# A one-core hybrid attention and retention block: sums of the first modulation tiles moved to TensorE, and wider feature jobs in the first half of the input projection

## The reference

```
mod = c @ w_ada + b_ada                        # (1, 2048) @ (2048, 6*2048): 100 MB of weights
sh1, sc1, gt1, sh2, sc2, gt2 = split(mod, 6)
h = rmsnorm(x, g_mix) * (1 + sc1) + sh1        # x is (256, 2048)
proj = h @ w_in                                # 2048 x 5376
qa, ka, va, qr, kr, vr, gr = split(proj)       # 1024, 128, 128, 1024, 1024, 1024, 1024 columns
ya = sliding_window_attention(qa, ka, va, sinks) * beta_attn
yr = silu(gr) * head_group_norm(retention(qr, kr, vr), g_ret)
x = x + gt1 * (concat(ya, yr) @ w_out)         # 2048 x 2048
h2 = rmsnorm(x, g_ffn) * (1 + sc2) + sh2
x = x + gt2 * (square(relu(h2 @ w1)) @ w2)     # 2048 x 8192, 8192 x 2048
return rmsnorm(x, g_final)
```

## Time and profile before

| | |
|---|---|
| median of 3 runs | 1197.4 us (1197.1 to 1199.3) |
| profiled execution, its own time | 1198.7 us |
| span from first to last instruction in it | 1196.9 us |
| TensorE busy | 1128.5 us, 94% |
| VectorE busy | 808.2 us, 68% |
| ScalarE busy | 490.6 us, 41% |
| mean DMA rate over the span | 253 GB/s |
| HBM read | 300.2 MB |
| TensorE's first product with `w_in` | starts at 67.6 us |

### The profile page before, as it was taken

One profiled execution on the slowest core, in us unless ns is written; L12 is line 12 of the kernel. 1 busy time (PEld: TensorE's weight loads), 2 busy tenths in 40 slices (PEclk: granted clock), 3 DMA queues, 4 the chain that ended last, 5 costly groups with the idle time before them and its releaser, 6 DMA issues.

```text
span 1196.9 us, 15614 instructions
## 1 busy us (share of the span) xinstructions
PE 1128.5 (94%) x6235; PEld 963.2 (80%) x6235; DVE 808.2 (68%) x653; ACT 490.6 (41%) x495; POOL 19.1 (2%) x23
## 2 busy tenths in 40 slices
PE   0489999999999999999999999999999999999996
PEld 0489989888778778888888888888888888888884
DVE  5877767988776978875656566655656555665675
ACT  2233444554543445444333444333444333444442
POOL 2000001000000000100000000000000000000000
PEclk9779999999999999999999999999999999999998
DMA  9999988899997866767666667666666665665541
GB/s 363 402 331 332 361 295 296 317 363 385 354 407 298 293 218 234 233 189 266 225 235 187 186 190 255 239 217 200 185 205 245 217 240 182 188 194 182 190 155 71
DMA packets 152250, 302.94 MB, mean 253 GB/s; under 512 B 5088, under 2 KB 73296, under 8 KB 143632
## 3 DMA queue, kind: packets, MB, share of 16 engines
q1 hardware_dynamic: 150880, 298.08, 71.4%
q10 hardware_dynamic: 832, 2.93, 0.6%
q0 software_dynamic: 496, 1.35, 0.3%
HBM read 300.24 MB, written 2.10 MB: 253 GB/s over the span
## 4 chain that ended last, share of the span: by engine, by line
PE 87%; DVE 8%; DMA 3%; issue 1%; ACT 0%; ACTq 0%; DVEq 0%; SPq 0%
PE ps_job L765 18%; PE ps_job L800 14%; PE ps_job L802 14%; PE ps_job L801 14%; PE ps_job L768 9%; PE ps_job L780 4%; PE ps_job L781 4%; PE ps_job L782 4%; DVE acc L1045 3%; DVE w_lo L1105 2%; PE ps L864 1%; DMA stage<-in_w_ada 1%; DMA gate_rows<-in_w_ada 1%; PE ps L742 1%; DMA cst<-in_consts 1%
## 5 line engine op out<-in xcount | busy, mean ns | idle before, releaser
L1105 DVE TENSOR_TENSOR w_lo<-stage,w_hi 128x2048 fp32r<-128x2048 f32 x186 | 426.2, 2291 | 244.2 <-ACT w_hi L453 244.1
L453 ACT ACTIVATE w_hi<-stage 128x2048 fp32r<-128x2048 f32 x186 | 356.1, 1915 | 512.4 <-PE ps_job L802 309.4
L765 PE MATMUL ps_job<-act_hl,w_hi 128*128 128x512 f32 x1024 | 322.2, 396 | 2.3 <-DVE w_lo L1105 1.6
L768 PEld LDWEIGHTS ps_job<-act_hl,w_lo 128*128 128x128 f32 x1024 | 192.4, 188 | 45.4
L768 PE MATMUL ps_job<-act_hl,w_lo 128*128 128x256 f32 x1024 | 201.2, 278 | 0.0
L800 PE MATMUL ps_job<-w_hi,hid_hl 128*128 128x512 f32 x512 | 200.8, 392 | 0.0
L801 PE MATMUL ps_job<-w_lo,hid_hl 128*128 128x512 f32 x512 | 199.3, 389 | 0.0
L802 PE MATMUL ps_job<-w_hi,hid_hl 128*128 128x512 f32 x512 | 199.2, 389 | 0.0
L765 PEld LDWEIGHTS ps_job<-act_hl,w_hi 128*128 128x128 f32 x1024 | 156.1, 189 | 3.3 <-issue 1.8
L1045 DVE SCALAR_TENSOR_TENSOR acc<-stage,small,acc 128x2048 f32<-128x2048 f32 x64 | 150.3, 2348 | 5.7 <-DMA stage<-in_w_ada 2.6
L801 PEld LDWEIGHTS ps_job<-w_lo,hid_hl 128*128 128x128 f32 x512 | 96.1, 188 | 20.8 <-issue 1.0
(11 more groups left out here) (170 smaller groups left out, 788.4 us busy)
## 6 DMA issues: line engine op xcount, KB each, us to landing
stage<-in_w SPq DMA_DIRECT2D x128, 1024.0 KB, 5.4
stage<-in_w_ada SPq DMA_DIRECT2D x80, 1024.0 KB, 7.2
stage<-in_w_in SPq DMA_DIRECT2D x42, 1024.0 KB, 6.3
stage<-in_w_out SPq DMA_DIRECT2D x16, 1024.0 KB, 8.4
gate_rows<-in_w_ada SPq DMA_DIRECT2D x16, 1024.0 KB, 7.1
x_sb<-in_x ACTq DMA_DIRECT2D x1, 2048.0 KB, 14.2
out_y<-f_acc SPq DMA_DIRECT2D x3, 512.0 KB, 4.3
acc<-in_g_final POOLq DMA_DIRECT2D x1, 1024.0 KB, 7.4
```

What stands on the lines that cost most here:

```text
L453: nc.scalar.activation(w_hi[:, ring, :], stage[:, slot, :], ACT.Copy).then_inc(hi_ready, 1)
L765: nc.tensor.matmul(ps_job[:, 2 * pair + e, :], w_hi[:, ring, ws], act_hl[:, kt, :], start=(kt == 0), stop=False)
L768: last = nc.tensor.matmul(ps_job[:, 2 * pair + e, T:2 * T], w_lo[:, ring, ws], act_hl[:, kt, 0:T], start=False, stop=(kt == KT - 1))
L1105: nc.vector.tensor_tensor(w_lo[:, ring, :], stage[:, slot, :], w_hi[:, ring, :].bitcast(F32), ALU.subtract).then_inc(lo_ready, 1)
```

## The change

1. **Sums of the first 16 tiles on TensorE.** `sum_early` multiplies each tile, in four quarters of 512 columns, with `c` spread over 32 stationary columns, and sums the four quarters in the four 32-partition strips of PSUM bank `ps_job[3]`: 64 float32 matmuls. Tiles 0 to 4 come before `turn_normed`, 5 to 15 behind it. The slots come free by a semaphore of their own (`tile_summed`); `lo_ready` counts from item 16 on. The bias comes by four broadcast DMAs from POOL's queue to a 128 x 512 buffer `early_sums`; DVE adds the bank to it (one instruction) and TensorE turns the result with four small matmuls (`turn_quarters`). DVE has no tile to sum in the head.
2. **Piecewise modulation.** The k-tiles become ready in pieces of 2, 2, 4, 4 and 4 (`CHUNKS`), and the narrow group goes through its k-tiles in order and waits piece by piece. In the first half DVE modulates the first piece and ACT the others. DVE's split of group 0 stands between its modulation and the tails.
3. **The second sum** is cut up: after group 17 four float32 matmuls with `ones` as 32 stationary columns (`sum_quarters`), a copy by DVE, and `turn_quarters` within group 18, behind its first six matmuls.
4. **Broad jobs.** In the first half three jobs of 1024 columns (four groups of two k-tiles, still 48 matmuls of 256 columns a group) stand for the six wide ones; they use `ps`, `ps_job`, `ps` in turn, and ACT copies each out with one instruction of 2048 elements per partition. A group's DMA rows grow from 2 KB to 4 KB.
5. **Tiles 16 to 31** come one before each group from group 3 on, rather than seven in eight from group 1 on.

The core of the diff:

```diff
+JOBS = [("feat", KV0, 0, HALF)] + feature_jobs("broad", BROAD_COLS, 0) + token_jobs(0)
...
-PRE = 5 * KT
+PRE = 4 * KT
+BIASES = (None, 32, 48, 16)
+CHUNKS = [(0, 2), (2, 2), (4, 4), (8, 4), (12, 4)]
+EARLY_CHUNKS = 3
...
-    return KT + min(KT, (7 * g + 6) // 8) + min(2 * KT, max(0, (g - SUM_FROM) * 8 // 9))
+    return KT + min(KT, max(0, g - 2)) + min(2 * KT, max(0, (g - SUM_FROM) * 8 // 9))
...
+READY = [max(0, i + 1 - KT) for i in range(len(ITEMS))]
...
+            if JOBS[j][0] == "broad":
+                return [4 * (j % 2) + n for n in range(4)]
...
-                load_group(src, i % SLOTS, i - SLOTS + 1)
+                if SLOTS <= i < KT + SLOTS:
+                    sp.wait_ge(tile_summed, i - SLOTS + 1)
+                load_group(src, i % SLOTS, READY[i - SLOTS] if i >= KT + SLOTS else 0)
...
+            for n in range(STRIPS):
+                col = (SH1, SC1)[n // 2] + TOK_COLS * (n % 2)
+                pool.dma_start(early_sums[32 * n:32 * n + 32, :], b_ada[0:1, col:col + TOK_COLS].to_broadcast([32, TOK_COLS])).then_inc(early_loaded, 16)
...
             static_group(0)
             act.wait_ge(squares, 2)
-            modulated_head(0)
+            act.wait_ge(mod_ready, 1)
+            modulated_head(*CHUNKS[0])
+            for k, n in CHUNKS[1:EARLY_CHUNKS]:
+                modulate(k, n)
+                modulated_head(k, n)
             static_group(1)
...
+            def sum_early(k):
+
+                item = ITEM_OF_TILE[k]
+                pe.wait_ge(stage_full[item % SLOTS], 16 * (item // SLOTS + 1))
+                for n in range(STRIPS):
+                    last = nc.tensor.matmul(ps_job[32 * n:32 * n + 32, 3, :], vec_T[:, V_C + k:V_C + k + 1].to_broadcast([P, 32]),
+                                            stage[:, item % SLOTS, n * TOK_COLS:(n + 1) * TOK_COLS], start=(k == 0), stop=(k == KT - 1))
+                last.then_inc(tile_summed, 1)
+
+            pe.wait_ge(vec_ready, 1)
+            for k in range(5):
+                sum_early(k)
             pe.wait_ge(normed, 1)
             turn_normed()
+            for k in range(5, KT):
+                sum_early(k)
...
+            def sum_quarters(a, bank):
+
+                for n in range(STRIPS):
+                    last = nc.tensor.matmul(ps[32 * n:32 * n + 32, bank, :], ones[:, 0:32], acc[:, a, n * TOK_COLS:(n + 1) * TOK_COLS],
+                                            start=True, stop=True)
+                last.then_inc(quarters_summed, 1)
+
+            def turn_quarters(bank):
+
+                for m in range(4):
+                    o = ps[:, bank, 0:KT].rearrange("p (n m) -> p n m", m=4)[:, :, m]
+                    last = nc.tensor.matmul(o, early_sums[:, m * P:(m + 1) * P], ident.rearrange("p (n c) -> p n c", c=32)[:, :, 0], start=True, stop=True)
+                last.then_inc(mod_summed, 1)
...
-            pe.wait_ge(lo_ready, ITEM_OF_TILE[KT - 1] + 1)
-            sum_mod(0, 0, 0)
+            pe.wait_ge(early_added, 1)
+            turn_quarters(0)
...
+                for k in range(8):
+                    if chunk + 1 < len(CHUNKS) and k0 + k == CHUNKS[chunk + 1][0]:
+                        chunk += 1
+                        pe.wait_ge(act_ready, chunk + 1)
...
+                        if half_turn and (k, t) == (0, TT - 1):
+                            pe.wait_ge(quarters_copied, 1)
+                            turn_quarters(2)
...
                     if g == 0:
-                        pe.wait_ge(act_ready, 2)
+                        pe.wait_ge(act_ready, 1)
                     if g == G_B:
-                        pe.wait_ge(act_ready, 4)
+                        pe.wait_ge(act_ready, EARLY_CHUNKS + 1)
...
                     if g == G_B - 2:
-                        pe.wait_ge(lo_ready, ITEM_OF_TILE[2 * KT - 1] + 1)
-                        sum_mod(1, 2, 0)
+                        pe.wait_ge(lo_ready, READY[ITEM_OF_TILE[2 * KT - 1]])
+                        sum_quarters(1, 3)
...
-            split_group(0, ITEM_OF_GROUP[0] % SLOTS, 0, 1)
+            dve.wait_ge(tile_summed, KT)
+            dve.wait_ge(early_loaded, 64)
+            nc.vector.tensor_tensor(early_sums[:, :], early_sums[:, :], ps_job[:, 3, :], ALU.add).then_inc(early_added, 1)
             take_modulation(0)
             dve.wait_ge(turned_out, 8)
...
+            for k in range(CHUNKS[0][1]):
+                nc.vector.tensor_scalar(xn_T[:, k, :], xn_T[:, k, :], scale1[:, k:k + 1], shift1[:, k:k + 1],
+                                        ALU.mult, ALU.add).then_inc(h_ready, 1)
+            split_group(0, ITEM_OF_GROUP[0] % SLOTS, 0, 1)
...
                     if g == G_B - 1:
+                        dve.wait_ge(quarters_summed, 1)
+                        nc.vector.tensor_copy(early_sums[:, :], ps[:, 3, :]).then_inc(quarters_copied, 1)
                         take_modulation(1)
```

More of the change, by code:

```diff
@@ L32 @@
 TOK_COLS = 512
+BROAD_COLS = 1024
 STRIPS = D // TOK_COLS
@@ L66 @@
 J_MLP = J_OR + STRIPS
-N_GROUPS = [nk // (8 if kind == "feat" else 4) for kind, _, _, nk in JOBS]
+N_GROUPS = [nk // {"feat": 8, "broad": 2}.get(kind, 4) for kind, _, _, nk in JOBS]
 FIRST = [sum(N_GROUPS[:j]) for j in range(len(JOBS) + 1)]
@@ L272, in result_of @@
                 return k_dup[:, :, :]
+            tiles = BROAD_COLS // P if kind == "broad" else TOK_COLS // P
             if c0 < KV0:
-                return q_T[:, c0 // P:c0 // P + 4, :]
-            if kind == "wide":
-                return qk_ret[:, (c0 - QR0) // P:(c0 - QR0) // P + 4, :]
+                return q_T[:, c0 // P:c0 // P + tiles, :]
+            if c0 < VR0:
+                return qk_ret[:, (c0 - QR0) // P:(c0 - QR0) // P + tiles, :]
             if c0 < GR0:
@@ L866, in row_sums, with sum_mod @@
                 last.then_inc(rows_summed, 1)
+            def sum_mod(a, bank):
+                for k in range(KT):
+                    last = nc.tensor.matmul(ps[:, bank, k:k + 1], acc[:, a, k * P:(k + 1) * P], ones[:, 0:1], start=True, stop=True)
+                last.then_inc(mod_summed, 1)
             def turn_rows():
@@ L920, in _ @@
                     if kind == "feat":
-                        half_feature_group(j, k0, g % 2)
+                        narrow_group(k0, g % 2, banks(j)[0], EARLY_CHUNKS if j else 0)
+                    elif kind == "broad":
+                        broad_group(k0 + 2 * q, g % 2, ps if j % 2 else ps_job, q == 0, q == N_GROUPS[j] - 1)
                     elif kind == "wide":
```

150 lines of the change are left out of this document (78 added, 72 removed).

## The result

The changed kernel takes **1191.0 us** (median of 5 runs, 1188.4 to 1192.0); the kernel before, run beside it, 1197.6. The ratio is 0.994, with an interval of 0.9925 to 0.9956: 6.6 us faster, where 7.1 were forecast. The profiled execution took 1191.9 us and its span is 1189.8, which is the number the working came to.

A forecast was written before the change was run, and what follows sets the result against it. TensorE, busy 94% of the span, was taken as the bound. Head 6.6 plus turn 0.5 gave 7.1 us, span 1196.9 to 1189.8, forecast 1190.3 us against the median 1197.4; range 1186.5 to 1194.5.

The forecast's parts named there:

- Bound and place: Whole kernel: TensorE, busy 94% of the span, bounds it; gains come in head and turn, no TensorE gap until group 17 ends.
- From the landing of tile 15 to the first product: Head: tile 15's sum, addition, turning, shift and scale, modulation, split and tail run from 52.2 to 61.0 us.
- The landing itself: Head: four broadcast DMAs, 0.26 MB at 408 GB/s, delay tile 15 by 0.6 us, to 52.2.
- Group 0's clock: Head: group 0 takes 7.8 us, as it did, if the clock rises as late as it did.
- The turn: End of group 17 to group 19: start 2.0 us earlier, less 1.5 for a clock fall; 0.5 gained, bounds 0 and 2.0.
- The head: Start to first product: it moves from 67.6 to 61.0 us, 6.6 us gained; upper bound 8.0.
- the forecast's own marks for "wrong": DMA dip at 35 to 42 us, ACT waiting for DMA, group 1 over 1.5 us from 68.9, slower bank changes, new late waits.
- Warmer clock: Head and turn: full clock until tile 15 and free idle time at the turn give 10.0 us, about 1187.4; chance 0.2.
- TensorE in the way: Head: sums 5 and later wait behind turning x; eight slow rounds, 13.3 us, make everything 3.7 later: 1194.0; chance 0.08.
- Given back: Near 340 to 360 us: loads really hold the pace, so TensorE waits there for what it gained: 1197; chance 0.06.
- starved: From group 3: loads at 318 GB/s lose 14.9 us, 1205, chance 0.05; in part, near 1193.5, chance 0.06.

The follow-up runs named there:

- second profile of before: The unchanged kernel before, profiled once more to see what scatters in its trace: 1196.3 us (one run), span 1194.4.
- wide jobs: Changed kernel with the six wide jobs of 512 columns in the first half instead of three broad ones: 1190.1 us, ratio 0.9942.
- added work: Changed kernel with x's turning rounds spread behind tile sums 5 to 12, bias in single rows, and unread matmuls in head, turn and behind group 52: 1187.1 us.
- warm turn: Changed kernel with three matmuls that nobody reads behind group 18, where TensorE idles: 1191.2 us, ratio 0.9942.
- second sum as before: Changed kernel, but the second sum is sixteen one-column matmuls between groups 17 and 18, without copy or turning: 1191.9 us, ratio 0.995.
- new sums without pieces: Changed kernel, but narrow groups 0 and 19 wait for all pieces of the modulation before their first matmul: 1197.4 us, ratio 0.9996.
- pieces without new sums: Changed kernel, but DVE sums the first tiles and both column sums are sixteen one-column matmuls; modulation pieces and broad jobs stay: 1196.0 us, ratio 0.9989.
- bias rows: Changed kernel, but the bias of the first sums comes by four one-row loads into zeroed memory instead of four broadcasts: 1189.9 us, ratio 0.9928.
- warmed head: Changed kernel with unread matmuls, one behind each of tile sums 10 to 14 and three behind the first turning: 1188.5 us, ratio 0.9921.
- dealt-out rounds: Changed kernel with the eight rounds that turn x placed one behind each of tile sums 5 to 12, not all ahead of sum 5: 1189.3 us, ratio 0.9929.
- DVE's sums: Changed kernel, but DVE sums the first 16 tiles as in the kernel before, with column sums in quarters: 1190.8 us, ratio 0.9942.

## Why the prediction was right, and where not

**Bound and place.** Right: TensorE is the bound, the gain lies in the head and the turn, and TensorE has no gap between groups 1 and 17.

**From the landing of tile 15 to the first product:** 8.8 us forecast (52.2 to 61.0), 8.9 measured (53.2 to 62.1). Sum 1.9 at half clock, addition 0.7, turning 1.9, modulation 0.7, split 2.3 on the path and tail 0.6 are all within 0.1 us of their rows. Every one had a row of before with the same shape.

**The landing itself** was mis-sized: 0.6 us of delay from the byte count of the broadcasts, 1.7 measured, and the named cause was wrong. The broadcasts' delay is gone by tile 15; 0.9 of the 1.7 goes with an instruction packet, and 0.8 stays open. The trace of before could not show a packet whose place moves with the code.

**Group 0's clock** was mis-sized too. The working said 7.8 us "if the clock rises as late as it did"; it rose 1.7 us later in the group, and the group took 8.5. The condition was written down, but no price put beside it. Together: 6.6 - 1.0 - 0.1 - 0.8 = 4.7.

**The turn** was right in size: group 19 after 10.2 us forecast, 10.2 measured; idle time 2.9 forecast, 2.6 measured; the clock fell, for 3.4 us; net 0.5 forecast, 0.44 measured. The last match is partly luck: both the 12.2 us of before and the net gain hang on where the clock fell, and in the second profile of before the stretch is 11.6 us (12.3 in the first by the same reading), and the net gain against it is 1.2.

**Why the total still fits.** The head gave 1.9 us less than forecast; the clock at 434 us and a DMA wait at 510 us of the profiled execution of before gave back 2.0 that the sum did not have. By the medians the gain is 6.6 us, between the 5.1 of head and turn and the 7.1 of the spans. So the direction and about five of the seven microseconds are explained by the steps; the head and the turn have 5.1 us against either profile of before. The rest of the profiles' difference is in places that the change did not touch. How much of the 6.6 us between the medians is the clock was not separated; against the median of all fifteen runs of before, 1196.8, they are 5.8. Of the forecast's own marks for "wrong", two were there: group 1 started at 70.7, not within 1.5 us of 68.9, and the DMA rate dipped at 38 to 44 us.

**The rivals.** *Warmer clock* came true in part, run by run: in the profile with wide jobs group 21 is 8.4 us ahead of before, and with added work 10.1. *TensorE in the way*: the dip was there, with the turning 9.3 us long where the rival's eight slow rounds had 13.3; its cost was not. *Given back* and *starved* did not happen: TensorE never waited for a load of these groups. The Trainium skill (DMA: Bandwidth & Descriptors, "Where 436 GB/s comes from") gets its limit of about 358 GB/s per core by halving what two cores share. One core is at work here, and this trace lies above that figure again: 368 GB/s over 20 us and 397 over another 20.

## What to carry to other kernels

When a step on the way to the bottleneck engine's first work is cut, cut the one behind it as well: at group 2 new sums and piecewise modulation gave 4.7 us together, 2.4 and 1.2 each alone, and in the totals 6.6 together and under 2 each alone. Then try the parts of the change one by one: here the largest, the tile sums on TensorE, had nothing of the total. Cost such a chain from rows of the same shape at the clock that the engine will have there, and put a price on every "if the clock stays" as on any other term. Before crediting a fraction of a per cent to a change, compare two profiles of the unchanged kernel: here they differ by 2.5 us.

## What the runs showed of the hardware that was not expected

- The granted clock fell for 3.4 us behind idle time of 2.1 to 2.6 us, but not each time. Behind the same 2.09 us before group 53 it fell in the first profile of before and in four of the changed ones (warm turn, second sum as before, new sums without pieces, pieces without new sums), and not in the second of before, the kernel after and five others. Behind the same 2.6 us at the turn it fell in the kernel after, with bias rows and with the warmed head, and not with wide jobs, dealt-out rounds and DVE's sums. After 3.75 us of idle time it fell 1.1 us into group 19:

```profile
177.00:181.00 4.00, 0.25 (x2) 0.20 (x2) 2.68 (x3) 4.00 (x5) 0.03 (x1) 1.00 0.70 248
```

  That is the kernel without pieces: idle for 3.75 of 4 us with the granted clock at 1.00; its half clock came from 181.9 to 185.3.
- Work whose result nobody reads made the kernel faster: in the head 2.0 us by the profile and 2.5 by the medians, over all places 3.9 us together with bias rows and dealt-out rounds.
- Behind one instruction packet of 16 KB (1.08 us, the time of one DMA engine of 16) the next tile landed about 0.9 us late, in nine traces (0.7 to 1.3), and so did those behind it; where the packet came 0.8 us later, the delay came one tile later.
- A delay of 1.7 us in the landing of tile 1, which the broadcasts made, made no difference at tile 15 (53.2 with them, 53.3 without): here bytes ahead in the queues were no measure of how late the last load lands.
